# High and low parts in the projections of the two latent layers' mixers

## The reference, cut to what matters

```python
def modulate_2(x, shift, scale):
    return rms_norm(x) * (1 + scale) + shift

for l in range(DEPTH_2):                  # 2 layers
    hx = modulate_2(x, sh1, sc1)          # 1024 x 1024
    hc = modulate_2(xc, csh1, csc1)       # 256 x 1024
    px = hx @ w_in[l]                     # 1216 columns: u 256, v 256, f 256, q 256, kv 128, kr 64
    pc = hc @ w_in[l][:, col0:]           # last layer: only kv and kr
    # chunk_mlp(u, v), fourier_mix(f), attention over q, kv, kr; then w_out, then the experts
    v = rms_norm(gelu(pv)) * sgu_norm     # inside chunk_mlp
```

## Time and profile before

| | |
|---|---|
| three runs | 5121.59, 5125.55, 5130.87 us |
| profiled execution, its time | 5131.66 us |
| its span | 5129.9 us |
| PE busy | 4588.4 us (89%) |
| DVE busy | 2097.6 us (41%) |
| ACT busy | 1388.1 us (27%) |
| POOL busy | 971.9 us (19%) |
| mean granted TensorE clock | 0.931 of 2.4 GHz |

### The profile page before, as it was taken

The page is one execution under the profiler, slowest core; times in us unless marked ns, Lnnn a source line. Parts: engine busy times, 40 slices in busy tenths (PEclk is TensorE's granted clock), DMA queues, the critical chain, the costliest instruction groups (busy, mean ns, idle before and its releaser), DMA issues. The chain is left out here.

```text
span 5129.9 us, 87113 instructions
## 1 busy us (share of the span) xinstructions
PE 4588.4 (89%) x38086; PEld 3507.0 (68%) x38086; DVE 2097.6 (41%) x2937; ACT 1388.1 (27%) x2044; POOL 971.9 (19%) x706
## 2 busy tenths in 40 slices
PE   6989897899988889999979899888999789998797
PEld 3868776799974568888856567664555466676676
DVE  2027444444443242432330234436665212443886
ACT  2115112222221120000031223224554211232675
POOL 2310113344431123333300000011221001001111
PEclk9999997999998989999989799988999897999898
DMA  7210200000017211111120100047886210002898
GB/s 269 93 43 1 54 19 25 3 4 4 4 61 280 85 34 45 49 49 49 41 91 25 41 1 1 25 161 268 273 271 199 73 33 20 1 17 103 286 383 294
DMA packets 323241, 484.36 MB, mean 94 GB/s; under 512 B 43809, under 2 KB 199418, under 8 KB 313698
## 3 DMA queue, kind: packets, MB, share of 16 engines
q1 hardware_dynamic: 302434, 403.80, 22.7%
q0 software_dynamic: 17024, 63.11, 4.5%
q10 hardware_dynamic: 3456, 12.58, 0.6%
HBM read 422.81 MB, written 56.62 MB: 93 GB/s over the span
## 5 line engine op out<-in xcount | busy, mean ns | idle before, releaser
L3738 DVE TENSOR_TENSOR l_experts_lo<-l_raw_room,l_experts_hi 128x1024 fp32r<-128x1024 f32 x256 | 299.4, 1220 | 51.6 <-ACT l_experts_hi L3677 50.5
L3677 ACT ACTIVATE l_experts_hi<-l_raw_room 128x1024 fp32r<-128x1024 f32 x256 | 254.6, 1057 | 49.9 <-PEq L66 30.6
L2397 PE MATMUL l_in_bank<-l_mixT,l_in_w 128*128 128x512 f32 (+1 forms) x672 | 255.1, 542 | 0.6 <-issue 0.3
L2397 PEld LDWEIGHTS l_in_bank<-l_mixT,l_in_w 128*128 128x128 f32 x672 | 127.6, 190 | 127.6 <-issue 119.2
L142 PE MATMUL mlp_ps<-h_hi,mlp_w_hi 128*128 128x512 f32 x512 | 201.5, 394 | 7.6 <-DVE h_lo L531 6.8
L142 PE MATMUL mlp_ps<-h_lo,mlp_w_hi 128*128 128x512 f32 x512 | 199.7, 390 | 0.0
L142 PE MATMUL mlp_ps<-h_hi,mlp_w_lo 128*128 128x512 f32 x512 | 199.7, 390 | 0.0
L1721 POOL TENSOR_TENSOR rec_lv<-rec_ab,rec_masks 128x512 f32<-128x512 f32 x120 | 145.1, 1225 | 237.5 <-DVE rec_ab L1638 149.3
L3738 DVE TENSOR_TENSOR l_experts_lo<-l_experts_raw_down,l_experts_hi 128x1024 fp32r<-128x1024 f32 x128 | 153.2, 1223 | 85.0 <-ACT l_experts_hi L3677 84.5
L2297 ACT ACTIVATE mlp_hid_hi<-mlp_pos 128x1024 f32 x32 | 34.0, 1063 | 568.7 <-DVE mlp_pos L2311 568.7
L142 PE MATMUL mlp_ps<-mlp_hid_hi,mlp_w_hi 128*128 128x512 f32 x448 | 174.3, 389 | 0.0
(11 more groups left out here) (691 smaller groups left out, 11239.2 us busy)
## 6 DMA issues: line engine op xcount, KB each, us to landing
l_raw_room<-in_w_gate_dram SPq DMA_DIRECT2D x128, 512.0 KB, 5.4
l_raw_room<-in_w_up_dram SPq DMA_DIRECT2D x128, 512.0 KB, 7.2
l_experts_raw_down<-in_w_down_dram SPq DMA_DIRECT2D x64, 1024.0 KB, 6.5
rec_out_w_ada<-in_w_ada_dram SPq DMA_DIRECT2D x24, 1024.0 KB, 12.4
mlp_w<-in_w_mlp_up_dram SPq DMA_DIRECT2D x32, 512.0 KB, 3.8
mlp_w<-in_w_mlp_down_dram SPq DMA_DIRECT2D x32, 512.0 KB, 3.4
l_choose_w_ada<-in_w_ada_dram POOLq DMA_DIRECT2D x16, 1024.0 KB, 16.6
s_acc<-l_choose_zero SPq DMA_DIRECT2D x18, 512.0 KB, 5.6
```

The source lines that it names most:

```text
L2397: mm = nc.tensor.matmul(ps[:, m % 2, c, 0:n], w[:, m % 2, k], hT[:, k, t0:t0 + n], start=(k == 0), stop=(k == KT - 1))
L3677: nc.scalar.activation(hi[:, q % RING], piece(e, u), ACT.Copy).then_inc(hi_done, 1)
L3738: nc.vector.tensor_tensor(lo[:, q % RING], piece(e, u), hi[:, q % RING].bitcast(F32), ALU.subtract).then_inc(lo_done, 1)
```

## The change

`project_mixers` goes over to the split form. `mixT` no longer holds the norm's result; the stage has its own `h_hi` and `h_lo` (2 x 40 KB a partition), allocated from the other end of SBUF, and `mixT` is allocated there after the stage. The norm's work buffers become `fT` and `pq`, the experts' rows lie in `uT`, `vn`, `kvr` and one new buffer. The split norm loses the whole copy: DVE multiplies x by gain and inverse root in one operation per feature tile, ACT makes only the high part (bias alone), and DVE computes value + shift - high in one operation. This is also the norm of the MLP stage. Tiles 0 and 1 are both multiplied along with the norm, tile 1 in banks 7, 3 and 4. v takes its weights through the same two slots, as tiles 8 and 9. Of the rows of order below, the second fence of each pair has the line numbers of the changed program.

```diff
 class Norm: modulate (ACT)
-                        self.nc.scalar.activation(self.whole[u % len(self.whole)][:, 0:w], x, ACT.Identity, **form)
-                        self.nc.scalar.activation(dst[0][:, k, t], x, ACT.Identity, **form).then_inc(self.hi_done, 1)
+                        self.nc.scalar.activation(dst[0][:, k, t], x, ACT.Identity, bias=shift[:, k:k + 1]
+                                                  ).then_inc(self.hi_done, 1)
 class Norm: scale (DVE), rest
-                self.nc.vector.tensor_tensor(lo[:, k, t], self.whole[u % len(self.whole)][:, 0:w], hi[:, k, t].bitcast(F32),
-                                             ALU.subtract).then_inc(self.lo_done, 1)
+                self.nc.vector.scalar_tensor_tensor(lo[:, k, t], self.work[q % 4][:, j, 0:w], shift[:, k:k + 1],
+                                                    hi[:, k, t].bitcast(F32), ALU.add, ALU.subtract
+                                                    ).then_inc(self.lo_done, 1)
 class Norm: scale (DVE)
+                if self.split:
+                    dve.wait_ge(self.gain_done, len(self.groups))
+                    for j in range(2):
+                        last = self.nc.vector.scalar_tensor_tensor(
+                            self.work[q % 4][:, j, 0:w], self.groups[n][0][:, 2 * p + j, c0:c0 + w],
+                            self.gain[:, n, 2 * p + j:2 * p + j + 1], self.bc[:, m, 0:w], ALU.mult, ALU.mult)
+                    last.then_inc(self.scaled, 1)
+                    if q:
+                        rest(q - 1)
+                    continue
 project_mixers
-        w = s.sb("w", [P, 2, KT, P])
-        wv = s.sb("wv", [P, KT, SGU_W])
+        h = tuple(s.sb(x, [P, KT, T], F32R, RIGHT) for x in ("h_hi", "h_lo"))
...
+        FIRST = [[bank[:, c] for c in (0, 1, 2)], [bank[:, c] for c in (7, 3, 4)]]
...
+        w = SplitWeights(nc, s, KT, mul_done, 1)
...
+            @block.gpsimd
+            def _(pool):
+                for m in range(len(TILES) + 2):
+                    w.split(pool, m % 2, m // 2, full=16 * (m // 2 + 1) + (16 if m in (7, 9) else 0))
...
+                for b in range(2):
+                    pe.wait_ge(w.split_done[b], 1)
+                for c, (t0, n) in enumerate(spans):
+                    if c:
+                        pe.wait_ge(norm.scaled, c * norm.PAIRS)
+                    for k in range(KT):
+                        pe.wait_ge(norm.lo_done, c * KT + k + 1)
+                        for b in range(2):
+                            for j, (x, y) in enumerate(((w.hi, h[0]), (w.hi, h[1]), (w.lo, h[0]))):
+                                mm = nc.tensor.matmul(FIRST[b][c][:, 0:n], x[:, b, k], y[:, k, t0:t0 + n],
+                                                      start=(k + j == 0), stop=(k == KT - 1 and j == 2))
+                            if (c, k) == (len(spans) - 1, KT - 1):
+                                mm.then_inc(mul_done[b], 1)
+                pe.wait_ge(norm.lo_done, len(CHUNKS) * KT)
                 for m, (_, spn, _, _) in enumerate(TILES):
                     if m >= 2:
                         pe.wait_ge(read, m - 1)
...
+                        w.multiply(pe, m % 2, m // 2, h, KT, spn, ps[:, m % 2])
-                pe.wait_ge(v_loaded, 16)
+                for b in range(2):
+                    pe.wait_ge(w.split_done[b], 5)
+                pe.wait_ge(read, len(TILES))
                 for t in range(rows):
...
                     for k in range(KT):
-                        mm = nc.tensor.matmul(pv[:, t % 2, 0:SGU_W], hT[:, k, t * P:(t + 1) * P], wv[:, k],
-                                              start=(k == 0), stop=(k == KT - 1))
+                        for j, (x, y) in enumerate(((h[0], w.hi), (h[0], w.lo), (h[1], w.hi))):
+                            mm = nc.tensor.matmul(pv[:, t % 2, 0:SGU_W].rearrange("p (b c) -> p b c", b=2),
+                                                  x[:, k, t * P:(t + 1) * P], y[:, :, k],
+                                                  start=(k + j == 0), stop=(k == KT - 1 and j == 2))
```

More of the change, by code:

```diff
@@ L395, with __init__ @@
     PAIRS = KT // 2
-    def __init__(self, nc, s, ones, ident, groups, g_vec, ss, bc, work=None, whole=None):
+    def __init__(self, nc, s, ones, ident, groups, g_vec, ss, bc, work=None):
         self.nc, self.ones, self.ident, self.groups, self.g_vec, self.ss, self.bc = (nc, ones, ident, groups, g_vec,
@@ L407, in __init__ @@
             work = [room[:, b] for b in range(4)]
-        if whole is None and self.split:
-            room = s.sb("norm_whole", [P, 4, 512])
-            whole = [room[:, b] for b in range(4)]
-        self.work, self.whole, self.rs = work, whole, s.sb("norm_rs", [P, self.TT])
+        self.work, self.rs = work, s.sb("norm_rs", [P, self.TT])
         self.g_loaded, self.squared, self.added, self.summed, self.mean_done = (
@@ L527, in rest @@
             hi, lo = self.groups[n][3]
+            shift = self.groups[n][4]
             for j in range(2):
@@ L550, in scale @@
                                              ).then_inc(self.scaled, 1)
-                if self.split and q:
-                    rest(q - 1)
         if self.split:
@@ L557, with __init__ @@
 class ExpertSums:
-    def __init__(self, nc, s, ident, acc, gates, norm, banks):
+    def __init__(self, nc, s, ident, acc, gates, norm, banks, rooms):
         self.nc, self.ident, self.acc, self.gates, self.norm, self.banks = nc, ident, acc, gates, norm, banks
-        self.rows = s.sb("rows", [P, 8, D])
+        more = s.sb("rows", [P, 2, D])
+        self.rows = [*rooms, more[:, 0], more[:, 1]]
+        assert len(self.rows) == 8
         self.tiles = [(k, t0, n) for t0, n in CHUNKS for k in range(KT)]
@@ L2213, in mlp @@
         w = SplitWeights(nc, s, KT, ps_full, 1)
-        own = s.sb("norm_room", [P, 4, 512])
+        own = s.sb("norm_room", [P, 2, 512])
         norm = Norm(nc, s, ones, ident, groups, g_vec, ss, bc,
-                    [x.rearrange("p (a t) -> p a t", a=2) for x in (pos[:, 0], pos[:, 1], sq[:],
-                                                                    flat(own[:, 0:2]))],
-                    [own[:, 2], own[:, 3]])
+                    [x.rearrange("p (a t) -> p a t", a=2) for x in (pos[:, 0], pos[:, 1], sq[:], flat(own[:]))])
         def tiles(eng, step_up, step_down):
@@ L2333, with project_mixers @@
 MIX_F, MIX_Q = 512, 768
-def project_mixers(nc, name, ones, ident, groups, sums_of, w_in, tokens, uT, vn, fT, pq, kv, kr):
-    hT = groups[0][3]
+def project_mixers(nc, name, ones, ident, groups, sums_of, w_in, tokens, uT, vn, fT, pq, kvr):
     spans = [x for x in CHUNKS if x[0] < tokens]
@@ L2414, in _ @@
                 for m, (_, spn, dst, func) in enumerate(TILES):
-                    act.wait_ge(mul_done, m + 1)
+                    act.wait_ge(mul_done[m % 2], m // 2 + 1)
                     n = spn[-1][0] + spn[-1][1]
-                    nc.scalar.activation(dst[:, 0:n], ps[:, m % 2].rearrange("p c t -> p (c t)")[:, 0:n], func
-                                         ).then_inc(read, 1)
+                    if m == 1:
+                        nc.scalar.activation(dst[:, 0:512], FIRST[1][0], func)
+                        last = nc.scalar.activation(dst[:, 512:n], bank[:, 3:5].rearrange("p c t -> p (c t)")[:, 0:n - 512],
+                                                    func)
+                    else:
+                        last = nc.scalar.activation(dst[:, 0:n], ps[:, m % 2].rearrange("p c t -> p (c t)")[:, 0:n], func)
+                    last.then_inc(read, 1)
                 for t in range(rows):
@@ L3812, in second_layer @@
             uT, fT, vn = sb(tmp, "uT", [P, 2, T]), sb(tmp, "fT", [P, 2, T]), sb(tmp, "vn", [P, T // P, SGU_W])
-            project_mixers(nc, nm + "in", ones, ident, groups, sums_of, w_in, tokens, uT, vn, fT, pq, kv[:, 0], kr)
+            project_mixers(nc, nm + "in", ones, ident, groups, sums_of, w_in, tokens, uT, vn, fT, pq, kvr)
+            mixT = sb(mixing, "mixT", [P, KT, T], side=RIGHT)
             gate_and_fourier(nc, nm + "mix", cst, ones, ident,
```

61 lines of the change are left out of this document (26 added, 35 removed).

## The result

| | kernel before | changed kernel |
|---|---|---|
| median (lowest to highest) | 5126.44 us (5121.59 to 5131.13), 5 runs | 5098.2 us (5094.28 to 5109.06), 5 runs |
| profiled execution: time, span | 5131.66, 5129.9 us | 5098.2, 5096.4 us |

The ratio is 0.9945, 95% interval 0.9933 to 0.9958: the change makes the kernel 28 us faster, 33.5 us between the two profiled executions. The forecast was 5090, range 5075 to 5108.

A forecast was written before the change was run, and what follows sets the result against it. PE's column tiles were taken to bound both mixer stages. 61.6 - 2.0 - 14.1 - 7.8 - 6.2 + 4.5 = 36.0 us off the median of 5125.55 gives 5089.6, say 5090 us; range 5075 to 5108.

The forecast's parts named there:

- cheaper product: Both mixer stages: the split product shortens PE's tiles and v's steps, 33.0 us in the first, 28.6 in the second.
- start beside the norm: Start of PE's tiles in both mixer stages: four DVE operations and one low part come first, costing 1.0 us each.
- waits for POOL: Before tile 2 and before v in both mixer stages: PE waits for POOL's weight split, four gaps of 3.52 us.
- clock behind the gaps: Behind those four gaps PE's granted clock falls, costing 1.95 us each, bounds 0 and 2.35.
- POOL beside the sums: POOL's first splits slow DVE's additions of squares, 4.7 us in the first mixer stage and 1.5 in the second.
- MLP stage: The MLP's norm, with two ACT activations per pair instead of four, lets PE's first tile end 4.5 us earlier.
- v's rival: v's steps in both stages: two blocks of 128 columns cost double, 52 us more, 5141 us; chance 0.03.
- a low part takes 0.60, a pair 2.52 us, PE stays the bound by a little: Tiles 0 and 1 beside the norm: DVE needs 2.52 us a pair, PE 2.72, so both tiles keep full pace.
- a slow low part (1.28 us): Beside the norm: DVE cannot feed two tiles, a pair costs 3.88 us, kernel 5125 us, no change; chance 0.11.
- a clock that stays low: First two tiles of both mixer stages run at low clock, 49.3 us lost, kernel 5139 us; chance 0.04.
- DVE is idle there and takes nothing from it: At the four gaps: DVE does not slow POOL's split, so each gap is POOL's 3.52 us.

The follow-up runs named there:

- late_wait: Changed kernel with PE's wait for the context's low parts moved, in the second mixer stage, from before tile 2 to before tile 6; 5087.18 us, one run.
- the late split: Changed kernel with POOL splitting the first two tiles' weights, in both mixer stages, only after DVE's last additions of squares; 5091.48 us, ratio 0.9931.
- one_along: Changed kernel with one tile multiplied beside the norm instead of two, tile 1 computed behind tile 0; 5116.88 us, one run.

## Why the forecast held, and where it missed

The mechanism held, stage by stage. The size did not come out so well: the stages gain 30.3 us where 36.0 were forecast, and the medians 28. That this lies inside the range owes something to its width.

| term | forecast | measured |
|---|---|---|
| cheaper product | 61.6 | 33.0 in the first stage as forecast (13.78, 2.87 us); second 26.4, 2.2 short (11.20 and 14.0 for 10.87 and 13.79) |
| start beside the norm | -2.0 | -2.4 (PE 3.5 us behind DVE in both stages, 2.3 before) |
| waits for POOL | -14.1 | 3.4 + 3.7 + 7.0 + 3.7 = -17.8 |
| clock behind the gaps | -7.8 | -8.2 |
| POOL beside the sums | -6.2 | -5.1 in the first stage, +0.1 in the second |
| PE's first tile in the second stage | not counted | +0.7 |
| MLP stage | +4.5 | +3.4 |

*The cheaper product* was right as a mechanism and, in the first stage, as a size: a pace read from another stage with the same shapes carried over to 0.01 us. v's rival (two blocks of 128 columns costing double) fell at 2.87 us a step. In the second stage the borrowed pace was 0.33 us too short for every 1,024 tokens. Against that stands a little that I had not counted: the kernel before lost time at the beginning of this phase. ACT read its tile 1 there 30.75 us behind the first scaling, 0.97 more than PE's start (2.32) and two paces of 13.73; in the first stage the same sum leaves 0.27. The changed kernel lost 0.2 in both stages, so some 0.7 us are to its good. The low clock that the kernel before shows in 4028 to 4033 us (0.67) is not the reason in the main, for it lies ahead of the first tile, which starts at 4030.93:

```profile
4030.93:4036.00 5.07, 5.07 (x13) 2.44 (x13) 5.07 (x6) 5.07 (x8) 0.00 (x0) 0.97 0.01 2
```

*The start, and DVE's supply.* The step "a low part takes 0.60, a pair 2.52 us, PE stays the bound by a little" was off by 0.12 us a pair in its size, and PE's 2.72 still covers 2.64. The rivals of a slow low part (1.28 us) and of a clock that stays low are refuted, by 0.66 us and by a clock of 1.00 in both phases.

*Waits for POOL.* Each gap is POOL's 3.5 us, as forecast, and the third pair of buffers removed two of them in full and their clock with them, so that is shown. The step that failed is "DVE is idle there and takes nothing from it", which is true of the first stage. In the second it isn't idle: four low parts of the context are still to come, POOL blocks them, and PE waits for them although the next four tiles don't use them. That cost 3.5 us, and the second stage fell 3.7 short of its sum (15.2 worked out, 11.5 measured; with the terms as measured, 26.4 - 1.2 - 10.7 - 3.8 + 0.1 + 0.7 = 11.5). Moving the wait gave 3.0 of it back, and where DVE happened to end first the gap was 3.1 us as well.

*The clock* was priced from two gaps elsewhere at 1.95 us, and it cost 1.8 to 2.5 here. Over all runs a gap of 3.1 us or more cost 1.4 to 3.0: in late_wait and in the repeat of the changed kernel the gap before tile 2 of the first stage cost 3.0, above the forecast's upper bound of 2.35.

*POOL beside the sums* was priced from the MLP stage at 4.7 us for the first stage, and 5.1 came; the run with the late split shows that POOL was the cause. The 1.5 us for the second did not come: its six additions took 8.3 us instead of 7.3, but the first scaling came at 43.05 us behind the stage's start, 43.17 in the kernel before. In the repeat the additions took 10.3 us and the first scaling came at 44.01, so this term lies between 0 and 0.8.

*The MLP stage* gained by the mechanism named, alone too. Its size was 1.1 us short, 1.0 of it (16 x 0.06) for the 0.66 us of a low part.

Worked out, the stages gain 15.4 + 11.5 + 3.4 = 30.3 us, against 36.0. Between the two profiles 4.5 us more came from a place that the change doesn't touch, the final norm ahead of the first mixer stage. Its sums of squares on PE, in the changed kernel and in the one with the late split:

```profile
2600.32 1.99 PE L476 MATMUL norm_f_ss<-ones,norm_f_norm_work 128*128 128x1 f32 x16
```

```profile
2599.20 3.41 PE L476 MATMUL norm_f_ss<-ones,norm_f_norm_work 128*128 128x1 f32 x16
```

These are the same 16 matmuls in the same stage, once with the clock up and once with it down, 1.4 us apart; the 24 matmuls behind them take 2.78 and 5.35 us, another 2.6. In seven of the ten profiles the clock rose ahead of the sixteen and in three (the kernel before, that with only the norm changed, that with the late split) behind. From the MLP's first reading of a tile to the mixer's first square it is 725.7 to 726.5 us in the seven and 730.4 to 730.9 in the three. Since the late split has this stage's instructions word for word as the changed kernel has them, the change doesn't decide it; what does stays open. It makes the profiled difference (33.5 us) look nearer to the forecast than the stages are.

## What to carry to other kernels

A multiplication that gets cheaper turns the refill of its weight slots into the wait at each place where all slots come free at once; look for these places first (the start of a block that uses several, the end of a phase that uses two), and give them one slot more: here it was worth 18 us together with one wait moved, which alone gave 3.0; a third of the 18 was clock. Order POOL's work behind DVE's sums wherever both read SBUF and the result isn't needed yet. And a wait for "all of it" before a loop should stand before the first round that needs all of it: a quarter of a microsecond in the order of two engines decided over 3.5 us.

## What was not expected of the hardware

- Short gaps of PE cost little beyond themselves, longer ones did. Gaps of 1.2 and 1.65 us left the granted clock at 1.00, with 0.3 us lost behind them; gaps of 3.2, 3.4, 3.7 and 7.0 us were followed by 0.57, 0.72, 0.50 to 0.58 and 0.56, and 1.4 to 3.0 us were lost behind each, no more behind the 7.0 (1.7 to 2.1) than behind the 3.7 (1.4 to 2.6); one of 6.6 us in one_along cost 2.9.
- Where POOL's split met DVE's low parts, DVE paid nearly all of it: its four operations over 256 columns went from 1.66 to 7.2 us, one for each of POOL's four, and POOL's two tiles from 3.5 to 3.5 and 3.7 us. Each of the four ended 0.27 to 0.28 us behind one of POOL's.
- Matmuls over 512 columns in the same three products start every 0.227 us in the first mixer stage and every 0.233 us in the second, at a granted clock of 1.00 in both, and exchanging the places of the weight tiles did not exchange the paces. v's steps, over 256 columns, are no slower in the second stage: 2.84 us against 2.88.
